# Turned rows of the second MLP chunk in bank 0, and the last attention's gate columns made token by token

## The chip, the cores and the metric

The kernel runs on one NeuronCore of a Trainium2 chip. The metric is the device time of one execution in microseconds (us). Three timed runs of the kernel before are shown, and one further execution was profiled. TensorE is called PE here, its weight loads PEld, VectorE DVE, ScalarE ACT, GpSimd POOL. PSUM has eight banks of 128 x 512 fp32; every matmul writes into one of them, and ACT or DVE reads it from there.

## The reference, cut to what matters

Two blocks run one after the other on 256 tokens of width 1024. Two places matter here: the MLP of the first block and the gates of the last attention of the second block.

```python
# first block, its MLP (16 chunks of 256 hidden columns in the kernel)
h = rmsnorm(x, g_mlp[l])
hid = jnp.square(jax.nn.relu(jnp.einsum("bsd,df->bsf", h, w_mlp_in[l])))
x = x + jnp.einsum("bsf,fd->bsd", hid, w_mlp_out[l])
...
# second block, last attention: 16 heads, 3 gates for each head = 48 columns
h = post_norm(h, 0.5 * swiglu(...), ln_g[layer, 0], ln_b[layer, 0])   # norm 7 in the kernel
qg = h @ w_qg
q = qg[..., :N_HEADS * Dh].reshape(B, S, G, HG, Dh) * (Dh ** -0.5)
gates = jax.nn.sigmoid(qg[..., N_HEADS * Dh:]).reshape(B, S, G, HG, 3)
...
return g_b[..., 0:1] * o_c + g_b[..., 1:2] * o_s + g_b[..., 2:3] * o_w
```

## The kernel before

Everything is kept on the chip; only weights are streamed. Each weight unit (128 x 2048 fp32, or 128 x 384 for the gate columns `("qg", 0)`) is loaded by SP, rounded by ACT into a high part (line 1612) and completed by DVE with a low part (line 2103). A product is then made in three matmuls for each of the eight 128-row pieces of the 1024 inputs: high by high, high by low, low by high. Hence a product over all inputs is 24 matmuls of one form.

There are two forms. `up_T_split` keeps the weights stationary and moves the 256 tokens (`hT_hi`, `hT_lo`), and its result has features as rows. `up_tok_split` keeps 128 tokens stationary and moves the weight columns, and its result has tokens as rows. `hT_hi` and `hT_lo` are the normed activations turned to feature rows. They are made for each block `b` of 128 tokens and each half `h` of the features: PE turns four 128 x 128 pieces (`turn_rows`, line 811), ACT writes `hT_hi` (line 1667), DVE writes `hT_lo` (line 2215). `normed(n, b, k)` makes PE wait for the half that piece `k` belongs to.

Each engine runs its own hand-written order of instructions, and semaphores tie them together. The planner `plan_tiles` gives every PSUM tile a bank by its name. Most names take banks 0 to 3 in turn; some have a bank of their own. `open_tile(name)` makes PE wait until the tile that held this bank before has been read; `tile_copied(engine, name)` waits until the tile itself has been read.

Place one is the start of the first block's MLP, `mlp(2)`. The first two chunks are made token by token, so their hidden rows must be turned afterwards: `turn_hidden(c)` turns `hid` into the tile `("hm", c)`, ACT reads it (line 1800) and DVE reads it again (line 2479). The order on PE is: product down of chunk 0, `turn_hidden(1)`, the one small product `("rel",)` of 33 x 383 for a table, then the product up of chunk 2 into the tile `("m", 2)`. The chunk tiles `("m", c)` have bank `c % 3`, and `("hm", c)` has bank `3 - c`. So `("hm", 1)` and `("m", 2)` share bank 2.

Place two is the start of the last attention. After the last product of the swiglu, PE makes two small tiles `("ck",)` and `("cv",)` (4 and 32 small fp32 products; each fp32 product is two records in the trace), turns the two halves of token block 1 (`rest_of_norm(7)`), makes the 48 gate columns, and goes on to eight query tiles `queries(i)`. The gate columns are made by `up_T_split` as 48 rows of 256 tokens, in tile `("qg",)`. ACT applies tanh (line 1982) into `nsa_gT`. After `queries(3)` PE turns this back to token rows (`gate_rows`, tile `("qt",)`, two transposes of 48 x 128), and DVE finishes the gate from there (line 2751).

Of the kernel before, what the change touches and what calls it, by code (L numbers as in the profile page):

```python
# [29 lines left out]
P = 128  # L30
# [100 lines left out]
def plan_tiles():  # L131
# [7 lines left out]
    def half_norm(n, b):  # L139
        return [("n", n, b, h) for h in range(2)]  # L140
# [30 lines left out]
    third = ffn(2)  # L171
    names += [("cr", 0)] + [("ch", 0, m) for m in range(2)] + third[0:2]
    names += [("cr", 1)] + [("ch", 1, m) for m in range(2)] + third[2:]
    names += half_norm(7, 0) + [("ck",), ("cv",)] + half_norm(7, 1)

    def probs(i):
        return [("pt", i, p) for p in range(4)]

    names += [("qg",)] + [("q", i) for i in range(4)] + [("qt",), ("q", 4), ("cs", 0), ("q", 5)] + probs(0)
    names += [("q", 6), ("ct", 0), ("ov", 0), ("q", 7), ("cs", 1)]  # L180
    for i in range(1, N_PAIR):
        names += probs(i) + [("ov", i)]
# [4 lines left out]
    for seq, name in enumerate(names):  # L187
        if name[0] == "m":
            bank = name[1] % MLP_BODY
        elif name[0:2] == ("n", 2):  # L190
            bank = 2 + name[3]
        elif name[0] == "hm":
            bank = 3 - name[1]
        elif name[0] == "rel":
            bank = 3
        elif name[0] == "vec":
            bank = 5
        elif name == ("cr", 1):
            bank = 4
        elif name[0:2] == ("ch", 1):  # L200
            bank = 5 + name[2]
        elif name[0] == "ov" and name[1] < N_PAIR - 3:
            bank = 7
        else:
            bank, turn = turn % 4, turn + 1
        out[name] = (bank, held[bank], seq)
        held[bank] += 1
# [119 lines left out]
def two_blocks(nc, t, out):  # L327
    ctx = ExitStack()
    with ctx:
# [73 lines left out]
        def take(at, *shape, of=None):  # L403
            n = int(np.prod(shape))
            a = (arena if of is None else of)[:, at[0]:at[0] + n]
            at[0] += n
            if len(shape) == 1:
                return a
            names = "abcd"[:len(shape)]
            return a.rearrange("p (%s) -> p %s" % (" ".join(names), " ".join(names)),  # L410
                               **{x: s for x, s in zip(names[:-1], shape[:-1])})
# [61 lines left out]
        sc = take(at, 2, NB, 8, 16)  # L473
        cw2 = take(at, 2, 2, HD)
        nsa_g = take(at, NB, 3 * NH)
        nsa_gT = take(at, S)[0:3 * NH, :]

# [64 lines left out]
        def frees(name):  # L544
            return tile_read[TILES[name][0]]
# [238 lines left out]
        def _(pe):  # L784
# [12 lines left out]
            def open_tile(name):  # L797
                b, held, _ = TILES[name]
                if held:
                    pe.wait_ge(tile_read[b], held)  # L800
                return banks[b]

            def have(name):
                if name in SPLITS:
                    pe.wait_ge(split_ready, AHEAD + SPLITS[name] + 1)
                else:
                    u = UNITS[name]
                    pe.wait_ge(arrived[u % SLOTS], arrival(u))
# [9 lines left out]
            def up_T_split(o, unit, c0, n, norm=None, act=both_hT):  # L818


                for k in range(KT):
                    if norm is not None:
                        normed(norm, NB - 1, k)
                    for w, a, start, stop in passes(k, KT - 1):
                        ins = mm(o, unit[w][:, k, c0:c0 + n], act[a][:, k, :], start, stop)
                        if start:
                            settle(ins)
                return ins
# [508 lines left out]
            def rest_of_norm(n):  # L1337
                for h in range(2):
                    turn_rows(n, 1, h)
# [100 lines left out]
                                 m == 0, m == 1)  # L1440
            ins.then_inc(tile_done, 1)

            rest_of_norm(7)

            have(("qg", 0))
            o = open_tile(("qg",))
            up_T_split(o[0:3 * NH, 0:S], parts(("qg", 0), KT), 0, 3 * NH, 7).then_inc(tile_done, 1)
            owed[0] += 1

            def queries(i):  # L1450
# [1 line left out]
                o = open_tile(("q", i))  # L1452
                up_T_split(o[:, 0:S], parts(("q", i // 2), KT), i % 2 * P, P).then_inc(tile_done, 1)
                owed[0] += i % 2

            def gate_rows():
                tile_copied(pe, ("qg",))
                o = open_tile(("qt",))
                for b in range(NB):
                    ins = turn(o[:, b * 3 * NH:(b + 1) * 3 * NH], nsa_gT[:, b * P:(b + 1) * P], 3 * NH)  # L1460
                    settle(ins)
                ins.then_inc(tile_done, 1)

            def pair_scores(i, b):
                if b == 0:
# [69 lines left out]
            queries(0)  # L1535
            queries(1)
            queries(2)
            for name in (("kT", 2, 1), ("kT", 4, 1), ("kv", 5, 1), ("ck",), ("cv",)):
                tile_copied(pe, name)
            for k in (2, 3):  # L1540
                pe.wait_ge(k_swapped[k], 32)
            for b in range(NB):
                pair_scores(0, b)
            queries(3)
            gate_rows()
            queries(4)
            for b in range(NB):
                pair_scores(1, b)
# [38 lines left out]
        def _(act):  # L1587
# [391 lines left out]
                                     ACT.Copy)  # L1979
            ins.then_inc(frees(("cv",)), 1)  # L1980
            o = tile_ready(act, ("qg",))
            act.activation(nsa_gT, o[0:3 * NH, 0:S], ACT.Tanh, scale=0.5).then_inc(frees(("qg",)), 1)

            def queries(i):
                copy_tile(("q", i), qT[:, i, :], scale=HD ** -0.5)
# [81 lines left out]
        def _(dve):  # L2067
# [679 lines left out]
            for b in range(NB):  # L2747
                pair_maxima(0, b)
            low_unit(("q", 3))
            o = tile_ready(dve, ("qt",))  # L2750
            dve.tensor_scalar(nsa_g.rearrange("p b c -> p (b c)"), o[:, 0:NB * 3 * NH], 1.0, 0.5,
                              ALU.add, ALU.mult).then_inc(frees(("qt",)), 1)
            tile_copied(dve, ("qt",))
            dve.wait_ge(fills, 5)
            for b in range(NB):
                pair_maxima(1, b)
# [182 lines left out]
```

## Time and profile before

| | us |
|---|---|
| timed runs, median (lowest, highest) | 1442.28 (1440.83, 1442.69) |
| span of the profiled execution | 1440.7 |
| PE busy in it | 1414.5 |
| DVE busy in it | 933.1 |
| ACT busy in it | 659.0 |
| POOL busy in it | 76.9 |

The span runs from the first to the last instruction of the one profiled execution; the timed runs are other executions. The span is 1.5 us below the median of the timed runs. A row of a timeline gives the start, the time from the first start to the last end of what it merges, the engine and line, the operation, what it writes and reads, how many, and in square brackets how long the engine had been idle and who released it. A single matmul is shown for longer than it holds the array, since matmuls follow each other in a pipeline; the distance of two starts is its price.

### The profile page before, as it was taken

How to read it: one execution, taken by the hardware profiler on the slowest of the kernel's cores; microseconds unless marked ns; L12 is line 12 of the kernel's file. 1: busy time of each engine (PE TensorE's matmuls, PEld its weight loads, DVE VectorE, ACT ScalarE, POOL GpSimd, SP SyncE). 2: the span in 40 equal slices, each digit the busy share in tenths (PEclk: the TensorE clock that was granted, in tenths of full speed). 3: DMA queues.
4: the chain of work that ended last, by engine and by line, in shares of the span. 5: the costliest groups of instructions: out<-in, count | busy, mean ns of one | idle time of the engine just before them, and what ended most of it. 6: DMA issues, size and time to landing. Idle time of an engine off the chain costs nothing.

```text
span 1440.7 us, 25236 instructions
## 1 busy us (share of the span) xinstructions
PE 1414.5 (98%) x10426; PEld 1296.3 (90%) x10426; DVE 933.1 (65%) x1372; ACT 659.0 (46%) x833; POOL 76.9 (5%) x73
## 2 busy tenths in 40 slices
PE   8999999999999999999999999999999999999997
PEld 7989978989899999999889999999999887899996
DVE  6878586555665555758875556665555667755556
ACT  5665544343443444453343344444433468543432
POOL 0000140000100000000020000100000200100000
PEclk9999999999999999999999999999999999999999
DMA  8444564775657767564465656766656530566551
GB/s 276 151 133 128 192 205 155 226 235 188 206 188 238 260 199 224 176 191 165 162 208 188 202 187 210 252 198 206 204 177 202 156 118 27 178 207 199 191 188 59
DMA packets 191525, 268.41 MB, mean 186 GB/s; under 512 B 5740, under 2 KB 164752, under 8 KB 191182
## 3 DMA queue, kind: packets, MB, share of 16 engines
q1 hardware_dynamic: 186336, 250.05, 54.0%
q0 software_dynamic: 4224, 15.91, 3.2%
q10 hardware_dynamic: 878, 1.21, 0.3%
q8 instruction: 64, 1.05, 0.3%
q14 instruction: 23, 0.19, 0.0%
HBM read 261.92 MB, written 4.19 MB: 185 GB/s over the span
## 4 chain that ended last, share of the span: by engine, by line
PE 89%; DVE 7%; ACT 3%; issue 1%; DMA 1%; POOL 0%; SPq 0%; DVEq 0%
PE bank L788 87%; PE bank L811 2%; DVE split L2103 1%; DVE resid L2197 1%; DVE resid L2205 1%; DVE stats L2171 1%; DVE resid L2166 1%; DMA ring<-in_w_in 1%; ACT split L1612 1%; ACT arena L1993 0%; ACT act_out L2002 0%; ACT act_out L1635 0%; ACT arena L1685 0%; ACT xn L1993 0%; DVE hT_lo L2215 0%
## 5 line engine op out<-in xcount | busy, mean ns | idle before, releaser
L2103 DVE TENSOR_TENSOR split<-ring,split 128x2048 fp32r<-128x2048 f32 x217 | 496.1, 2289 | 341.0 <-ACT split L1612 340.5
L788 PE MATMUL bank<-hT_hi,split 128*128 128x256 f32 (+1 forms) x3984 | 700.5, 278 | 1.3 <-DVE hid_lo L2479 0.7
L788 PEld LDWEIGHTS bank<-hT_hi,split 128*128 128x128 f32 (+1 forms) x3984 | 607.7, 188 | 8.9 <-issue 4.7
L1612 ACT ACTIVATE split<-ring 128x2048 fp32r<-128x2048 f32 (+1 forms) x224 | 428.0, 1912 | 320.4 <-PE bank L788 315.1
L788 PE MATMUL bank<-hT_lo,split 128*128 128x256 f32 (+1 forms) x1992 | 552.1, 277 | 0.0
L788 PEld LDWEIGHTS bank<-hT_lo,split 128*128 128x128 f32 (+1 forms) x1992 | 374.5, 188 | 2.3
L788 PE MATMUL bank<-split,hid_hi 128*128 128x512 f32 x992 | 285.9, 394 | 0.1
L788 PEld LDWEIGHTS bank<-split,hid_hi 128*128 128x128 f32 x992 | 182.5, 188 | 38.0 <-issue 0.8
L788 PE MATMUL bank<-split,hT_hi 128*128 128x256 f32 (+1 forms) x896 | 172.2, 292 | 2.6 <-DVE hT_lo L2148 1.2
L788 PE MATMUL bank<-split,hid_lo 128*128 128x512 f32 x496 | 158.0, 392 | 0.0
L788 PEld LDWEIGHTS bank<-split,hT_hi 128*128 128x128 f32 x896 | 140.6, 188 | 10.1 <-issue 3.8
L788 PE MATMUL bank<-split,hT_lo 128*128 128x256 f32 (+1 forms) x448 | 127.1, 289 | 0.0
L1787 ACT ACTIVATE act_out<-bank 128x256 f32<-128x256 f32 (+1 forms) x104 | 43.5, 418 | 182.3 <-PE bank L788 182.2
L788 PEld LDWEIGHTS bank<-split,hid_lo 128*128 128x128 f32 x496 | 93.3, 188 | 20.6
L788 PEld LDWEIGHTS bank<-split,hT_lo 128*128 128x128 f32 x448 | 84.2, 188 | 1.9
L2805 POOL TENSOR_TENSOR split<-ring,split 128x2048 fp32r<-128x2048 f32 x7 | 32.6, 4663 | 736.1 <-ACT split L1612 519.6
L2449 DVE TENSOR_TENSOR hid_lo<-hid,hid_hi 128x256 fp32r<-128x256 f32 (+1 forms) x112 | 51.4, 459 | 3.8
L788 PE MATMUL bank<-arena 64*128 64x256 f32 (+6 forms) x442 | 50.2, 321 | 1.2 <-DVE neg_max L2688 0.8
L2548 DVE SCALAR_TENSOR_TENSOR hid<-act_out,bank 128x256 f32<-128x256 f32 x82 | 34.3, 419 | 24.0 <-ACT act_out L1787 24.0
L788 PEld LDWEIGHTS bank<-arena 64*128 64x128 f32 (+3 forms) x442 | 36.6, 168 | 11.2 <-issue 3.7
L2447 DVE CAST hid_hi<-hid 128x256 fp32r<-128x256 f32 (+1 forms) x112 | 34.8, 311 | 3.8
L1667 ACT ACTIVATE hT_hi<-bank 128x512 fp32r<-128x512 f32 x28 | 16.8, 599 | 39.9 <-PE bank L811 39.9
(217 smaller groups left out, 927.5 us busy)
## 6 DMA issues: line engine op xcount, KB each, us to landing
ring<-in_ffn_w SPq DMA_DIRECT2D x132, 1024.0 KB, 5.3
ring<-in_w_in SPq DMA_DIRECT2D x19, 1024.0 KB, 5.5
ring<-in_w_mlp_in SPq DMA_DIRECT2D x16, 1024.0 KB, 5.9
ring<-in_w_mlp_out SPq DMA_DIRECT2D x16, 1024.0 KB, 5.0
ring<-in_sgu_w_in SPq DMA_DIRECT2D x16, 1024.0 KB, 5.5
ring<-in_sgu_w_out SPq DMA_DIRECT2D x8, 1024.0 KB, 4.9
ring<-in_kv_w SPq DMA_DIRECT2D x6, 1024.0 KB, 6.2
ring<-in_w_out SPq DMA_DIRECT2D x4, 1024.0 KB, 5.3
```

The costliest lines, as they stand in the source:

```text
L788: ins = pe.matmul(o, lhsT, rhs, start=start, stop=stop)
L811: return pe.transpose(o, a, ident[0:n, 0:n])
L1612: act.activation(halves(q if i is None else q + BODY, n)[0], ring[:, u % SLOTS, 0:n], ACT.Copy).then_inc(hi_ready, 1)
L1667: act.activation(hT_hi[:, 4 * h:4 * h + 4, b * P:(b + 1) * P], o[:, :].rearrange("p (k s) -> p k s", k=4), ACT.Copy).then_inc(hT_rounded, 1)
L1787: act.activation(act_out[:, b, 0:cols], banks[b][:, 0:cols], func).then_inc(act_ready, 1)
L2103: dve.tensor_tensor(lo, ring[:, u % SLOTS, 0:n], hi.bitcast(F32), ALU.subtract).then_inc(split_ready, 1)
L2166: link(dve.scalar_tensor_tensor(out=r, in0=r, scalar=ALPHA if n >= 4 else 1.0, in1=acc[2 * b + h][:, :], op0=ALU.mult, op1=ALU.add))
L2171: link(dve.bn_stats(stats[:, b, h, :], resid[:, b, h * 512:(h + 1) * 512]))
L2447: dve.tensor_copy(hi, raw).then_inc(hid_rounded, 1)
L2449: return dve.tensor_tensor(lo, raw, hi.bitcast(F32), ALU.subtract)
L2548: dve.scalar_tensor_tensor(out=raw, in0=act_out[:, b, 0:S], scalar=0.5, in1=banks[b][:, S:2 * S], op0=ALU.mult, op1=ALU.mult).then_inc(til ...
L2805: pool.tensor_tensor(lo, ring[:, u % SLOTS, :], hi.bitcast(F32), ALU.subtract).then_inc(split_ready, 1)
```

## The change

The tile `("hm", 1)` gets bank 0 and not bank 2. `("hm", 0)` keeps bank 3.

The gate columns are made in the other form. The 128 tokens of a block are stationary and the 48 weight columns move, 24 matmuls for each of the two blocks, into columns 0 to 47 and 48 to 95 of one tile, in bank 4. The part for block 0 stands ahead of `rest_of_norm(7)`, the part for block 1 behind it. ACT's tanh reads the tile once and writes the gates where they stay. The transposes, their tile `("qt",)` and the buffer `nsa_gT` are gone, and DVE finishes the gates in place in SBUF, at the same place of its order. The name `("qg",)` and `("qt",)` no longer take one of the banks 0 to 3 in turn, so the tiles behind them move to other banks.

```diff
-    names += half_norm(7, 0) + [("ck",), ("cv",)] + half_norm(7, 1)
+    names += half_norm(7, 0) + [("ck",), ("cv",)] + half_norm(7, 1) + [("qg",)]
...
-    names += [("qg",)] + [("q", i) for i in range(4)] + [("qt",), ("q", 4), ("cs", 0), ("q", 5)] + probs(0)
+    names += [("q", i) for i in range(4)] + [("q", 4), ("cs", 0), ("q", 5)] + probs(0)
...
         elif name[0] == "hm":
-            bank = 3 - name[1]
+            bank = 0 if name[1] else 3
...
-        elif name == ("cr", 1):
+        elif name in (("cr", 1), ("qg",)):
             bank = 4
...
+            have(("qg", 0))
+            gates = open_tile(("qg",))
+            up_tok_split(gates[:, 0:3 * NH], parts(("qg", 0), KT), 3 * NH, 0, 7)
             rest_of_norm(7)
-
-            have(("qg", 0))
-            o = open_tile(("qg",))
-            up_T_split(o[0:3 * NH, 0:S], parts(("qg", 0), KT), 0, 3 * NH, 7).then_inc(tile_done, 1)
+            up_tok_split(gates[:, 3 * NH:6 * NH], parts(("qg", 0), KT), 3 * NH, 1, 7).then_inc(tile_done, 1)
             owed[0] += 1
...
-            def gate_rows():
-                tile_copied(pe, ("qg",))
-                o = open_tile(("qt",))
-                for b in range(NB):
-                    ins = turn(o[:, b * 3 * NH:(b + 1) * 3 * NH], nsa_gT[:, b * P:(b + 1) * P], 3 * NH)
-                    settle(ins)
-                ins.then_inc(tile_done, 1)
...
-            for name in (("kT", 2, 1), ("kT", 4, 1), ("kv", 5, 1), ("ck",), ("cv",)):
+            for name in (("kT", 2, 1), ("kT", 4, 1), ("kv", 5, 1), ("ck",), ("cv",), ("qg",)):
                 tile_copied(pe, name)
...
             queries(3)
-            gate_rows()
             queries(4)
...
             o = tile_ready(act, ("qg",))
-            act.activation(nsa_gT, o[0:3 * NH, 0:S], ACT.Tanh, scale=0.5).then_inc(frees(("qg",)), 1)
+            act.activation(nsa_g.rearrange("p b c -> p (b c)"), o[:, 0:NB * 3 * NH], ACT.Tanh,
+                           scale=0.5).then_inc(frees(("qg",)), 1)
...
-            o = tile_ready(dve, ("qt",))
-            dve.tensor_scalar(nsa_g.rearrange("p b c -> p (b c)"), o[:, 0:NB * 3 * NH], 1.0, 0.5,
-                              ALU.add, ALU.mult).then_inc(frees(("qt",)), 1)
-            tile_copied(dve, ("qt",))
+            tile_copied(dve, ("qg",))
+            link(dve.tensor_scalar(nsa_g, nsa_g, 1.0, 0.5, ALU.add, ALU.mult))
```

PE at place one, before: the four transposes of `("hm", 1)` and the first matmuls of chunk 2 (bank2), with the table product between them.

```order
L811 MATMUL bank2<-const,hid 128x128 [waits tile_read2,tile_read1]
L811 MATMUL bank2<-const,hid 128x128 x3
L788 MATMUL bank3<-arena 128x383 [waits tile_read3,rel_wide_ready,rel_in]
L788 MATMUL bank2<-hT_hi,split 128x256 [waits tile_read2,split_ready]
L788 MATMUL bank2<-hT_lo,split 128x256
```

The same rows after the change (the line numbers are one lower there).

```order
L810 MATMUL bank0<-const,hid 128x128 [waits tile_read0,tile_read1]
L810 MATMUL bank0<-const,hid 128x128 x3
L787 MATMUL bank3<-arena 128x383 [waits tile_read3,rel_wide_ready,rel_in]
L787 MATMUL bank2<-hT_hi,split 128x256 [waits tile_read2,split_ready]
L787 MATMUL bank2<-hT_lo,split 128x256
```

Nothing changes its place in the row. Only the bank of the transposes is another, and with it the reader that `tile_read2` of chunk 2 stands for.

PE at place two, before: the small products of `("cv",)` (32x64), the eight transposes of token block 1 (from `resid`), and the start of the gate rows (48x256).

```order
L788 MATMUL bank1<-arena 32x64 x31
L811 MATMUL bank2<-const,resid 128x128 [waits tile_read2,xn_ready]
L811 MATMUL bank2<-const,resid 128x128 x3
L811 MATMUL bank3<-const,resid 128x128 [waits tile_read3,xn_ready]
L811 MATMUL bank3<-const,resid 128x128 x3
L788 MATMUL bank0<-hT_hi,split 48x256 [waits tile_read2,tile_read0,split_ready]
L788 MATMUL bank0<-hT_lo,split 48x256
```

The same place after: the end of the gate columns of block 0, the transposes, and the start of those of block 1 (both 128x48).

```order
L787 MATMUL bank4<-split,hT_hi 128x48
L810 MATMUL bank2<-const,resid 128x128 [waits tile_read2,xn_ready]
L810 MATMUL bank2<-const,resid 128x128 x3
L810 MATMUL bank3<-const,resid 128x128 [waits tile_read3,xn_ready]
L810 MATMUL bank3<-const,resid 128x128 x3
L787 MATMUL bank4<-split,hT_hi 128x48 [waits tile_read2]
L787 MATMUL bank4<-split,hT_lo 128x48
```

24 matmuls of 128x48 now stand between the small products and the transposes, and 24 more behind the transposes take the place of the 24 of 48x256. The two 48-wide transposes between `queries(3)` and `queries(4)` are gone.

## Rows read from the trace of the kernel before

**Rows 1.** The page: span, busy time of the engines, and the chain by engine.

```profile
span 1440.7 us, 25236 instructions
PE 1414.5 (98%) x10426; PEld 1296.3 (90%) x10426; DVE 933.1 (65%) x1372; ACT 659.0 (46%) x833; POOL 76.9 (5%) x73
...
PE 89%; DVE 7%; ACT 3%; issue 1%; DMA 1%; POOL 0%; SPq 0%; DVEq 0%
```

**Rows 2.** Waits of PE: engine, line, for whom: total us, times, longest.

```profile
PE bank L811 <- DVE resid L2205: 3.2, 6, 0.9
...
PE bank L788 <- DVE hid_lo L2479: 0.7, 1, 0.7
```

**Rows 3.** Timeline at the second MLP chunk's turning.

```profile
235.58 0.60 PE L811 MATMUL bank<-const,hid 128*128 128x128 f32 x4
236.11 0.91 PE L788 MATMUL bank<-arena 33*128 33x383 f32 x2
236.22 0.60 ACT L1800 ACTIVATE hid_hi<-bank 128x512 fp32r<-128x512 f32 x1 [4.79 <-PE bank L811]
...
236.91 0.69 DVE L2479 TENSOR_TENSOR hid_lo<-bank,hid_hi 128x512 fp32r<-128x512 f32 x1 [1.94 <-ACT hid_hi L1800]
237.75 0.36 PE L788 MATMUL bank<-hT_hi,split 128*128 128x256 f32 x1 [0.73 <-DVE hid_lo L2479]
```

**Rows 4.** DVE's timeline ahead of that: the low part of chunk 2's weights.

```profile
229.88 2.29 DVE L2103 TENSOR_TENSOR split<-ring,split 128x2048 fp32r<-128x2048 f32 x1 [0.16 <-DVE hid_lo L2479]
```

**Rows 5.** Timeline: the small products, the turning of block 1, the gate rows.

```profile
1141.59 3.02 PEld L788 LDWEIGHTS bank<-arena 128*32 128x32 f32 x64 [0.17 <-issue]
1141.62 0.69 DVE L2215 TENSOR_TENSOR hT_lo<-bank,hT_hi 128x512 fp32r<-128x512 f32 x1
...
1145.70 0.66 PE L811 MATMUL bank<-const,resid 128*128 128x128 f32 x4 [0.93 <-DVE resid L2205]
1146.34 0.75 DVE L2205 SCALAR_TENSOR_TENSOR resid<-resid,rstd,gain_rows 128x512 f32<-128x512 f32 x1
1146.39 0.60 ACT L1667 ACTIVATE hT_hi<-bank 128x512 fp32r<-128x512 f32 x1 [1.85 <-PE bank L811]
1147.02 0.69 DVE L2215 TENSOR_TENSOR hT_lo<-bank,hT_hi 128x512 fp32r<-128x512 f32 x1
...
1147.15 0.83 PE L811 MATMUL bank<-const,resid 128*128 128x128 f32 x4 [0.79 <-DVE resid L2205]
...
1147.86 0.42 PE L788 MATMUL bank<-hT_hi,split 128*48 128x256 f32 x1
1148.02 0.60 ACT L1667 ACTIVATE hT_hi<-bank 128x512 fp32r<-128x512 f32 x1 [1.03 <-PE bank L811]
...
1148.65 0.69 DVE L2215 TENSOR_TENSOR hT_lo<-bank,hT_hi 128x512 fp32r<-128x512 f32 x1 [0.93 <-ACT hT_hi L1667]
```

**Rows 6.** DVE's timeline: the low part of the gate columns' weights (128 x 384).

```profile
1124.64 0.55 DVE L2103 TENSOR_TENSOR split<-ring,split 128x384 fp32r<-128x384 f32 x1
```

**Rows 7.** Stretches: length, busy (count) of PE, PEld, DVE, ACT, POOL, clock granted, DMA.

```profile
9.94:11.14 1.20, 1.20 (x11) 1.14 (x11) 0.92 (x2) 0.06 (x2) 0.00 (x0) 0.50 0.42 52
...
44.99:48.40 3.41, 2.12 (x18) 1.70 (x17) 2.19 (x1) 3.38 (x8) 0.00 (x0) 1.00 0.00 0
...
1144.61:1147.50 2.89, 1.17 (x10) 0.77 (x9) 2.79 (x6) 0.60 (x1) 0.11 (x1) 1.00 0.00 0
1147.50:1150.91 3.41, 3.41 (x18) 2.93 (x17) 2.48 (x3) 2.84 (x6) 2.78 (x4) 0.50 0.63 225
1150.91:1154.00 3.09, 3.09 (x29) 3.09 (x28) 0.63 (x1) 2.19 (x3) 0.00 (x0) 1.00 0.97 280
```

**Rows 8.** PE's timeline: last gate rows, first query matmuls; then around the gates' turning.

```profile
1150.43 0.41 PE L788 MATMUL bank<-hT_hi,split 128*48 128x256 f32 x1
1150.64 0.41 PE L788 MATMUL bank<-hT_lo,split 128*48 128x256 f32 x1
...
1151.93 0.39 PE L788 MATMUL bank<-hT_hi,split 128*48 128x256 f32 x2
1152.15 0.28 PE L788 MATMUL bank<-hT_lo,split 128*128 128x256 f32 x1
...
1165.51 0.28 PE L788 MATMUL bank<-hT_hi,split 128*128 128x256 f32 x1
1165.72 0.32 PE L811 MATMUL bank<-const,arena 48*128 48x48 f32 x2
1165.97 0.39 PE L788 MATMUL bank<-hT_hi,split 128*128 128x256 f32 x1
1166.19 0.28 PE L788 MATMUL bank<-hT_lo,split 128*128 128x256 f32 x1
```

**Rows 9.** PE's timeline: 128 stationary columns, 32 moving, later in the attention.

```profile
1189.88 1.84 PE L788 MATMUL bank<-arena 128*128 128x32 f32 x15
```

**Rows 10.** PE's timeline at the start, clock 0.50: transposes of two shapes.

```profile
8.07 1.94 PE L811 MATMUL bank<-const,xn 128*128 128x128 f32 x8 [2.63 <-DVE xn L2128]
9.94 1.27 PE L811 MATMUL bank<-const,shared_rows 19*128 19x19 f32 x10
```

**Rows 11.** ACT's timeline: gate tanh, and the later stretch where ACT leads.

```profile
1152.24 0.38 ACT L1982 ACTIVATE arena<-bank 48x256 f32<-48x256 f32 x1 [0.90 <-PE bank L788]
1152.52 1.91 ACT L1612 ACTIVATE split<-ring 128x2048 fp32r<-128x2048 f32 x1
...
1197.82 1.74 ACT L2002 ACTIVATE act_out<-bank 128x256 f32<-128x256 f32 x4 [0.62 <-PE bank L811]
```

More of the change, by code:

```diff
@@ L475, in two_blocks @@
         nsa_g = take(at, NB, 3 * NH)
-        nsa_gT = take(at, S)[0:3 * NH, :]
         rel_dram = nc.dram_tensor("rel_scratch", (NH, P, N_REL), F32, kind="Internal")
```

## The prediction

> **What bounds the kernel now.** I read the page first: PE is busy for 98% of the span and holds 89% of the chain that ended last [rows 1]. So time goes away only where PE stands still, works at a lower clock, or does less; work of ACT and DVE counts where it makes PE wait. The second view is the list of PE's waits [rows 2]. Two of its rows belong to this change: one wait of 0.7 us for the low part of hidden rows (line 2479), and the waits of transposes for the last norm step (line 2205). The third view is the timeline at these places [rows 3, 5, 8]. The fourth is the table of stretches with the granted clock [rows 7], which shows something that no wait shows: behind the turning of block 1 PE works for 3.41 us at a clock of 0.50, its lower level of 1.2 GHz, and is back at 2.4 GHz at 1150.9.
>
> **Part one, bank of the second chunk's turned rows.** The table product starts as two records at 236.11; the two take 0.91 us as shown, to 237.02. The first matmul of chunk 2 starts at 237.75, after 0.73 us of idle time that DVE's line 2479 ended [rows 3]. That instruction reads the turned rows from bank 2 (236.91 to 237.60), and chunk 2 writes bank 2. With the turned rows in bank 0 nothing of chunk 2's start depends on it. What is late next? The weights of chunk 2 were ready at 229.88 + 2.29 = 232.17 [rows 4], their tokens long before, so the next limit is PE itself. The table product's own pipeline lets its follower start slightly before its shown end, so the gain is between 0.73 and 0.8; I take **0.8 us off**. The transposes now need bank 0, whose tile was read before the turning itself could start (the hidden rows that are turned come from it or from its neighbour, chunk 1), so no wait takes the place. ACT and DVE read the same number of elements as before. The down product of chunk 1 needs this low part, but only after 48 matmuls of chunk 2, more than 5 us later.
>
> **Part two, the turning of the gates.** The last matmul of `queries(3)` starts at 1165.51, the two transposes stand at 1165.72, and the next query tile starts at 1165.97, with its second matmul at 1166.19 [rows 8]. Where query matmuls follow gate matmuls without a change of kind, the distance is 0.11 (1151.93 for two, then 1152.15) [rows 8]. So the turning costs 1165.97 - 1165.51 - 0.11 = 0.35 us, and 0.22 - 0.12 = 0.10 more in the slow first step behind it. **0.45 us off.** DVE's part (once from PSUM, now in SBUF) and ACT's tanh (0.38 us, [rows 11]) shrink or stay, and ACT waited 0.90 us for it. Both stay beside PE's work: no price.
>
> **Part three, the gate columns in the other form.** Before, 24 matmuls; after, 48, each with 128 stationary and 48 moving columns. No row of before has just that shape. The nearest is 128 stationary with 32 moving: 15 of them in 1.84 us, less some 0.28 for the last one's length, is 1.56 / 14 = **0.112 us each** [rows 9]. The other neighbour is 32 stationary with 64 moving: 64 in 3.02 us, 0.047 each [rows 5]. The first has the new one's stationary width, and its 32 columns alone cannot need 0.112, so it is the load that sets the pace; I take 0.112 and keep 0.047 for a rival.
>
> The Trainium skill (TensorE: Matmul & The Clock Gate, LDWEIGHTS) says the load's time goes with the number of stationary columns, not with the contraction; at its rate 128 columns take 107 ns, and the row agrees. The same page's table of back-to-back gaps puts a matmul of 1 to 64 moving columns at about 25 ns; by that the 48 would cost an estimated 1.2 us instead of 5.4. That is the rival below, priced there from rows.
>
> Now the places. Block 0's 24 take 24 x 0.112 = 2.69 us. Their inputs are there: `hT_lo` of block 0 ended at 1142.31 [rows 5], the weights at 1125.19 [rows 6]. They can start where the small products end; the last of these starts some 0.17 before the end of PE's busy time, 1145.70 - 0.93 = 1144.77 [rows 5]. So they run from 1144.61 to 1147.30. Before, this time held 0.93 + 0.79 us of waiting and four transposes. Both halves of block 1's rows are ready by then (1147.09), so eight transposes at 0.109 run to about 1148.2. Behind them, by the distances of before: ACT started 0.69 after the first of four transposes and 0.60 long; DVE ended at 1147.71, which is 2.01 after them; PE followed 0.15 later. So the first half is usable at 1147.30 + 2.01 + 0.10 + 0.15, about 1149.4-1149.5, and PE idles about 1.2 us. The second half is usable 0.7 later and not waited for, since 12 matmuls take 1.34. Block 1's 24 end at 1149.4 + 2.69 = **1152.1**, where the queries start. Before, they start at 1152.04 [rows 8]. **Against the profiled execution, all at full clock, part three is zero** (0.06).
>
> **What the clock does to this.** Before, the gate matmuls stand 0.21 apart at the low clock (1150.43, 1150.64) and 0.11 at the high one [rows 8]. At full clock they would have begun at 1147.83, waited for the second half (1148.65 + 0.69 + 0.15 = 1149.49) and ended at 1149.49 + 12 x 0.113 = 1150.85. So the low clock costs 1.19 of before's time, and clock against clock the new form is 1.25 us dearer: it does not fill a hole with useful work, it puts 2.7 us of extra work in a hole of 1.7 and opens one of 1.2.
>
> Will the clock fall again? The stretch 1144.61 to 1147.50, ahead of the fall, has PE busy for 1.17 of 2.89 us. A stretch with more transposes (44.99 to 48.40, busy 2.12 of 3.41) kept 1.00 [rows 7]. After the change PE is busy nearly throughout until 1148.2, which speaks for a full clock. Against it: at the start of the program ten transposes with 19 moving columns kept PE busy throughout from 9.94 to 11.14, and the clock stayed at 0.50 [rows 7, 10]. The change makes the stretch from 1144.6 to 1152.1 almost all of such narrow work: 48 narrow matmuls, eight transposes, a hole. I think it likelier that the clock falls again, and later than before, so that full-width query matmuls meet it. A stretch as long as the one before, 3.41 us, at half pace takes 1.7 us of them. The narrow ones lose little: the 19-wide transposes at the low clock stand at most 0.127 apart (1.27 / 10), near the 0.112.
>
> **Sum of the likeliest case:** -0.80 - 0.45 + 1.25 - 1.19 + 1.7 = **+0.5 us**. The profiled execution had the low stretch; its span is 1.5 below the median, which I take for what lies around the span, so I add to the median: 1442.28 + 0.5 = **1442.8 us**. Nothing absorbs it later: after the queries the chain stays on PE. At 1197.82, where ACT takes over the chain for 16 us, it had waited 0.62 for PE [rows 11], so a shift of part two's size passes.
>
> **Rivals.**
> - *The clock stays full.* The narrow matmuls close the hole ahead of the transposes, and the hole behind them is 1.2 us, no more than what 44.99 to 48.40 held (3.41 - 2.12 = 1.29) at full clock [rows 7]. Then -0.80 - 0.45 + 1.25 - 1.19 = -1.2, 1441.1 us.
> - *Narrow matmuls are cheap* (0.047 each). Block 0's end at 1145.74 and hardly delay the transposes; block 1's wait for the second half at about 1149.6 and end 12 x 0.047 later, 1150.15, that is 1.9 earlier than before. Sum -3.15, 1439.1 us. Against it stands the 0.112 of the 32-column row.
> - *Slower: the clock stays low over block 1's gates and a stretch of queries, and the narrow ones double too.* The place is 1149.4 on; full transposes at the low clock stand 0.213 apart (7 steps and one length in 1.94) [rows 10]. It decides from the point where a narrow matmul keeps that pace and not that of the 19-wide ones: 24 x 0.10 = 2.4 more, with 1.7 for the queries: -1.2 + 2.4 + 1.7 = +2.9, 1445.2 us.
> - *Part one brings nothing*, because chunk 2's start has another late input that the same 0.73 hid. Rows 4 speak against it. Then +0.8 on the forecast: 1443.6 us.
>
> **How the numbers follow.** Chances: likeliest case 0.45, full clock 0.32, cheap narrow ones 0.04, slow case 0.09, part one void 0.08, the rest 0.02. A measurement of this kernel can tell about 0.2%, 2.9 us, from no change: below 1439.4 is faster, above 1445.2 slower. Faster: the cheap case and little else, 0.05. Slower: about half of the slow case and a little scatter, 0.06. The rest, 0.89, is no change. The range goes from 1440.2 (the full-clock case, less the 0.9 that the runs of before scatter) to 1444.6 (the likeliest case with two low stretches of full matmuls, 1442.8 + 1.7, and 0.1). It leaves out the cheap case, the slow one and some scatter, about 0.17.
>
> **What would show it.** Part one: chunk 2's first matmul directly behind the table product, no idle for line 2479. Part two: no 48 x 48 transposes, query matmuls 0.11 apart through the seam. Part three: narrow matmuls 0.112 apart, transposes of block 1 some 1.6 us later against the small products, a hole of 1.2 us, queries 7.5 us after the last small product. The clock: one low stretch that begins behind the transposes; none would show the first rival. I am wrong if the narrow matmuls stand far from 0.112, if the hole is not there, or if a wait of ACT or DVE in the attention grows.

## The result, and the profile after

| | before | after |
|---|---|---|
| median, us (6 runs each) | 1442.35 | 1446.22 |
| lowest to highest | 1440.80 to 1442.77 | 1444.75 to 1447.06 |
| span of the profiled execution | 1440.7 | 1444.9 |

The ratio is 1.0032, with a 95% interval of 1.0021 to 1.0043. The kernel became slower by 3.9 us. The forecast was 1442.8 us and no change that can be told; the range ended at 1444.6. The measured 1446.22 also lies above 1445.2, where the prediction had put its bound for "slower" and had given that a chance of 0.06.

The page of the changed kernel has these lines for those of [rows 1]: the span, the busy times and the chain.

```profile
span 1444.9 us, 25267 instructions
PE 1421.4 (98%) x10448; PEld 1302.7 (90%) x10448; DVE 932.7 (65%) x1372; ACT 659.1 (46%) x833; POOL 76.9 (5%) x73
...
PE 87%; DVE 7%; ACT 3%; DMA 1%; issue 1%; POOL 0%; SPq 0%; DVEq 0%
```

PE was busy for 6.9 us more, with only 22 records more on the page. The other engines did the same as before. So work on PE took longer, and the waits do not tell why. In the list of PE's waits the 0.7 us for line 2479 [rows 2] has gone, the waits of transposes for the last norm step fell from 3.2 to 1.0 us, and only 0.6 us stands at the gate columns:

```profile
PE bank L787 <- DVE hT_lo L2206: 0.6, 1, 0.6
```

The table of stretches does tell. Its columns are as in [rows 7].

```profile
1143.32:1146.03 2.71, 2.71 (x27) 2.71 (x25) 2.32 (x4) 0.00 (x0) 0.02 (x1) 1.00 0.02 6
1146.03:1159.68 13.65, 13.09 (x62) 12.69 (x62) 5.87 (x4) 6.41 (x10) 2.86 (x4) 0.50 0.70 233
1159.68:1162.00 2.32, 2.32 (x22) 2.32 (x22) 0.00 (x0) 0.00 (x0) 0.00 (x0) 1.00 0.86 281
```

The clock was at its lower level, 1.2 GHz, for 13.65 us, four times as long as in [rows 7]. Ahead of the fall PE had been busy without a gap, with the 24 narrow matmuls of token block 0. The hole behind the turning comes only at 1147.98, 1.95 us after the fall, so it did not cause the fall. The timeline of PE, ACT and DVE at this place answers to [rows 5, 8]:

```profile
1143.32 0.29 PE L787 MATMUL bank<-split,hT_hi 128*128 128x48 f32 x1
...
1145.90 0.28 PE L787 MATMUL bank<-split,hT_hi 128*128 128x48 f32 x1
...
1146.02 1.97 PE L810 MATMUL bank<-const,resid 128*128 128x128 f32 x8
...
1147.80 0.69 DVE L2206 TENSOR_TENSOR hT_lo<-bank,hT_hi 128x512 fp32r<-128x512 f32 x1 [2.09 <-ACT hT_hi L1657]
...
1148.54 0.41 PE L787 MATMUL bank<-split,hT_hi 128*128 128x48 f32 x1 [0.56 <-DVE hT_lo L2206]
...
1153.47 0.39 PE L787 MATMUL bank<-split,hT_hi 128*128 128x48 f32 x1
1153.68 0.56 PE L787 MATMUL bank<-hT_hi,split 128*128 128x256 f32 x1
1154.04 0.41 PE L787 MATMUL bank<-hT_lo,split 128*128 128x256 f32 x1
```

Block 0's narrow matmuls: 23 steps from 1143.32 to 1145.90 are 0.112 each, as forecast. Block 1's: 23 steps from 1148.54 to 1153.47 are 0.214 each. The queries start at 1153.68 and run at half pace until 1159.68.

At place one the timeline answers to [rows 3]:

```profile
235.12 0.60 PE L810 MATMUL bank<-const,hid 128*128 128x128 f32 x4
235.65 0.91 PE L787 MATMUL bank<-arena 33*128 33x383 f32 x2
236.49 0.38 PE L787 MATMUL bank<-hT_hi,split 128*128 128x256 f32 x1
```

From the first transpose to chunk 2 it is 1.37 us where it was 2.17: 0.80 less.

**Where the time went, trace against trace.** The new trace reaches place one 0.46 earlier, which is not the change's doing. Place one gives 0.80. Between the two places 0.12 is gained. In the attention I measure from the start of the last small product to the start of the first product with 32 moving columns, read off single records: 26.95 us before, 32.55 after, so 5.60 lost. From there on the two agree within 0.02. Together -0.46 - 0.80 - 0.12 + 5.60 = +4.2, the difference of the spans. The 5.60 has three parts. The queries start 10.52 us after the last small product, not 7.48: +3.04. The first three query tiles take from 1153.68 to 1164.65 where they took from 1152.04 to 1160.09: +2.92. The rest of the way, with the seam without the turning, is 0.34 shorter, and the parts add up to 5.62.

### The profile page after: what moved, and what is told of

The parts are those of the page before. It is cut to its first block, busy times and chain, and to the rows that moved or that the text cites. A ratio compares the mean times of both kernels' runs of the same rounds, so it can differ in the third digit from the quotient of the medians.

```text
span 1444.9 us, 25267 instructions
## 1 busy us (share of the span) xinstructions
PE 1421.4 (98%) x10448; PEld 1302.7 (90%) x10448; DVE 932.7 (65%) x1372; ACT 659.1 (46%) x833; POOL 76.9 (5%) x73
## 4 chain that ended last, share of the span: by engine, by line
PE 87%; DVE 7%; ACT 3%; DMA 1%; issue 1%; POOL 0%; SPq 0%; DVEq 0%
PE bank L787 85%; PE bank L810 2%; DVE split L2094 1%; DMA ring<-in_w_in 1%; DVE resid L2188 1%; DVE resid L2196 1%; DVE stats L2162 1%; ACT split L1602 1%; DVE resid L2157 1%; ACT act_out L1625 0%; ACT arena L1984 0%; ACT act_out L1993 0%; ACT xn L1984 0%; DVE hT_lo L2206 0%; DVE shared_rows L2398 0%
## 5 line engine op out<-in xcount | busy, mean ns | idle before, releaser
L787 PE MATMUL bank<-hT_hi,split 128*128 128x256 f32 x3968 | 698.9, 278 | 0.5 <-DVE split L2094 0.4
L787 PEld LDWEIGHTS bank<-hT_hi,split 128*128 128x128 f32 x3968 | 607.5, 189 | 7.7 <-issue 3.7
L787 PE MATMUL bank<-hT_lo,split 128*128 128x256 f32 x1984 | 550.5, 277 | 0.0
L787 PEld LDWEIGHTS bank<-hT_lo,split 128*128 128x128 f32 x1984 | 374.4, 189 | 2.2
L787 PE MATMUL bank<-split,hT_hi 128*128 128x256 f32 (+2 forms) x928 | 179.7, 293 | 2.5 <-ACT act_out L1625 0.6
L787 PEld LDWEIGHTS bank<-split,hT_hi 128*128 128x128 f32 x928 | 147.4, 190 | 10.9 <-issue 3.8
L787 PE MATMUL bank<-split,hT_lo 128*128 128x256 f32 (+2 forms) x464 | 132.2, 290 | 0.0
L787 PEld LDWEIGHTS bank<-split,hT_lo 128*128 128x128 f32 x464 | 88.5, 191 | 1.9
```

The lines of the kernel that those rows point to most:

```text
L787: ins = pe.matmul(o, lhsT, rhs, start=start, stop=stop)
```

## The experiments

Each run was timed beside the kernel before. "Distance" is the one just defined: from the last small product to the first product with 32 moving columns. Before has 26.95, the change 32.55. "Low" is how long the clock was at 0.50 in the profiled execution, without the start and the end of the program.

| run | median us | before, beside it | ratio (95%) | distance | low near the gates |
|---|---|---|---|---|---|
| e1 part one alone | 1439.77 | 1441.47 | 0.9990 (0.9981 to 0.9999) | 27.08 | 3.41 |
| e2 gates alone | 1447.59 | 1441.47 | 1.0038 (1.0025 to 1.0052) | 31.14 | 10.24 |
| e3 wide moving | 1441.33 | 1441.47 | 0.9999 (0.9990 to 1.0008) | 26.84 | none |
| e4 change and fill | 1442.30 | 1441.47 | 1.0004 (0.9995 to 1.0013) | 26.64 | none |
| e5 old form and fill | 1439.64 | 1441.02 | 0.9988 (0.9980 to 0.9997) | 25.64 | none |
| e6 two halves | 1439.32 | 1441.02 | 0.9987 (0.9979 to 0.9996) | 25.05 | none |
| e7 all behind | 1447.10 | 1441.02 | 1.0042 (1.0029 to 1.0055) | 32.45 | 10.24 |
| e8 query first | 1442.70 | 1441.02 | 1.0010 (1.0001 to 1.0019) | 30.07 | 3.41 twice |
| e9 two halves and fill | 1439.86 | 1441.76 | 0.9985 (0.9976 to 0.9994) | 24.98 | none |
| e10 the change again | 1445.30 | 1441.76 | 1.0025 (1.0015 to 1.0034) | 31.12 | 10.24 |

### The two parts apart: e1 and e2

e1 has only this, e2 all but this:

```diff
-            bank = 3 - name[1]
+            bank = 0 if name[1] else 3
```

> The kernel before with part one alone: the turned rows of the second MLP chunk go to bank 0, the gate columns stay as they were. Theory (the whole loss is in the gate columns and the clock behind them): chunk 2's first matmul starts 1.37 us after the first turning transpose, not 2.17, and the time is 0.8 us below the kernel before, about 1441.5; the clock has one low stretch of 3.4 us at the gate rows, or none. Rival (part one also costs something, such as a wait later in the MLP): the time is at or above that of the kernel before.

> The changed kernel with part one undone: only the gate columns are changed. Theory: 0.8 us above the changed kernel, about 1447.0, with the clock low for some 10 to 14 us behind the transposes of token block 1 and the narrow matmuls there 0.213 us apart. Rival (part one carries the loss): about 1442.

e1's timeline at place one shows the 0.80 again (235.70 to 237.06 is 1.36).

```profile
235.70 0.60 PE L811 MATMUL bank<-const,hid 128*128 128x128 f32 x4
236.22 0.91 PE L788 MATMUL bank<-arena 33*128 33x383 f32 x2
237.06 0.39 PE L788 MATMUL bank<-hT_hi,split 128*128 128x256 f32 x1
```

e1's runs fall in two groups, six from 1439.33 to 1439.77 and five from 1440.83 to 1441.22. The profiled one is of the upper group and has the low stretch at the gate rows. That the lower group has none is inferred from its mean clock (0.995 to 0.998 there, 0.994 to 0.996 above, so the two overlap), not seen in a trace of e1. The groups stand 1.5 us apart. Part one is worth its 0.80 in the trace; the medians say 1.7, with an interval of 0.1 to 2.7. e2 carries the whole loss: 6.1 us above its own before, where the changed kernel was 3.9 above its own. The two intervals overlap, so they do not tell whether the difference is more than the 0.8 of part one; e2's trace has a second low stretch, at 214.47 to 217.89. The rival that part one hides a cost is out.

### The same work, but wide: e3

Same places, same number, same stationary operand. What moves is 256 columns of the query weights; the gates are not computed.

```diff
+            have(("q", 0))
...
-            up_tok_split(gates[:, 0:3 * NH], parts(("qg", 0), KT), 3 * NH, 0, 7)
+            up_tok_split(gates[:, 0:UC], parts(("q", 0), KT), UC, 0, 7)
             rest_of_norm(7)
-            up_tok_split(gates[:, 3 * NH:6 * NH], parts(("qg", 0), KT), 3 * NH, 1, 7).then_inc(tile_done, 1)
+            up_tok_split(gates[:, UC:2 * UC], parts(("q", 0), KT), UC, 1, 7).then_inc(tile_done, 1)
```

> The changed kernel with the same 48 matmuls at the same places and the same 128 stationary columns, but each moves 256 columns of the first query weights, not 48 gate columns; the gates are so left out of the result. At full clock both forms should stand 0.112 to 0.114 apart. Theory (a clock that falls and stays low because the matmuls are narrow): the clock is never low there, or for one stretch of 3.4 us, and the time is 1441 to 1442.5. Rival A (the hole of 1.2 us behind the transposes throws the clock): it falls as in the changed kernel and comes back one stretch later, 1443 to 1444. Rival B (the loss is the order of work and not the clock): 1446, as the changed kernel.

The stretches of e3: block 0's matmuls and the transposes, the hole, block 1's matmuls.

```profile
1143.48:1147.00 3.52, 3.52 (x33) 3.52 (x32) 2.33 (x4) 0.05 (x1) 0.82 (x2) 1.00 0.02 5
1147.00:1148.32 1.32, 0.35 (x4) 0.11 (x1) 0.74 (x2) 1.31 (x4) 1.32 (x3) 1.00 0.58 130
1148.32:1151.10 2.78, 2.77 (x23) 2.78 (x24) 2.75 (x2) 2.38 (x4) 0.75 (x1) 1.00 0.87 309
```

The hole is there: PE is busy for 0.35 of 1.32 us. The clock stays at 1.00. With five times the columns the kernel is 4 us faster than with 48, each against its own before. So the hole by itself does not do it, and neither does the order of work (rivals A and B). The price of such work at full clock is also seen: the distance is 26.84. The prediction's terms for full clock give 26.95 - 0.45 + 0.06 = 26.56.

### Full matmuls in the hole: e4

```diff
+            def fill(n, bank):
+                nil = zeros[:, :].bitcast(BF16)
+                for _ in range(n):
+                    settle(mm(bank[:, :], nil[:, 0:P], nil[:, 0:512], True, True))
...
             rest_of_norm(7)
+            fill(5, banks[7])
```

> The changed kernel with five full matmuls on zeros (512 moving columns, about 0.22 us each at full clock) put into the hole behind the transposes of token block 1; the narrow matmuls stay. Theory (the narrow matmuls hold the clock low): the clock still falls near the transposes and is low for 7 to 14 us, 1444.5 to 1446.5. Rival A (the hole throws the clock): it stays at full clock and the time is 1441 to 1442.

My theory missed here. The narrow matmuls are all there, and the clock stayed at 1.00 in the profiled execution. The last two lines are the timeline's: the turning and four of the five matmuls on zeros.

```profile
1143.70:1147.50 3.80, 3.79 (x34) 3.71 (x34) 2.32 (x4) 0.41 (x1) 1.11 (x3) 1.00 0.02 4
1147.50:1151.20 3.70, 3.66 (x29) 3.03 (x28) 3.48 (x3) 3.33 (x7) 1.77 (x2) 1.00 0.92 288
...
1146.40 1.09 PE L810 MATMUL bank<-const,resid 128*128 128x128 f32 x8
1147.54 1.03 PE L787 MATMUL bank<-zeros 128*128 128x512 bf16 x4
```

The eleven runs reach from 1440.84 to 1442.85; some may have had a low stretch. About 1.1 us of full matmuls on zeros made the changed kernel some 3 us faster, each against its own before. How they did it is not shown. They start only about 1147.3, and in the other traces of the changed gates the fall came at 1146.03 (the change), 1147.25 (e10, 0.2 us ahead of its hole) and 1149.73 (e2, 0.2 us into its hole), that is before the hole or hardly in it. In e4's profiled execution the fall stayed away although the work ahead of the zeros was the same as in e10. So the hole is not what brings the clock down in the changed kernel; whether it helps to keep it down is open.

### The place: e7 and e8

e7 puts both blocks' narrow matmuls behind the turning. e8 puts block 1's behind the first query tile.

```diff
 e7
+            rest_of_norm(7)
             up_tok_split(gates[:, 0:3 * NH], parts(("qg", 0), KT), 3 * NH, 0, 7)
-            rest_of_norm(7)
...
 e8
-            up_tok_split(gates[:, 3 * NH:6 * NH], parts(("qg", 0), KT), 3 * NH, 1, 7).then_inc(tile_done, 1)
-            owed[0] += 1
...
             queries(0)
+            up_tok_split(gates[:, 3 * NH:6 * NH], parts(("qg", 0), KT), 3 * NH, 1).then_inc(tile_done, 1)
+            owed[0] += 1
             queries(1)
```

> The changed kernel with the narrow matmuls of token block 0 moved behind the turning of token block 1, so that all 48 stand behind it; the form is that of the change. Theory (a long stretch of narrow matmuls holds the clock low, wherever the hole is): the two waits ahead of the turning are back, the clock falls there, and is low over all 48 narrow matmuls at 0.213 us each and some of the query matmuls: 13 to 17 us low, the distance 34 to 37 us, time 1447 to 1451. Rival (the hole of 1.2 us behind the turning made the loss, and it is filled here): one low stretch of 3.4 us at most, distance 28 to 30, time 1442 to 1443.

> The changed kernel with the narrow matmuls of token block 1 moved behind the first query tile, so that 24 full matmuls stand between the turning and them. Theory (once low, the clock comes back only when full matmuls have run, and the narrow ones only delay that): one low stretch of 3.4 us at most two, the distance from the last small product to the first product with 32 moving columns is 27.5 to 29.5 us where the changed kernel has 32.6, time 1441.5 to 1443.5. Rival (the clock falls on the narrow matmuls alone, so it falls again on the moved ones): a low stretch behind them as well, 30 us or more, 1444 and above.

e7: the turning and its two waits, then the stretches from the first narrow matmuls on.

```profile
1144.85 0.63 PE L810 MATMUL bank<-const,resid 128*128 128x128 f32 x4 [1.14 <-DVE resid L2196]
1146.10 0.66 PE L810 MATMUL bank<-const,resid 128*128 128x128 f32 x4 [0.62 <-DVE resid L2196]
...
1146.40:1148.38 1.98, 1.98 (x21) 1.98 (x20) 1.40 (x3) 1.57 (x4) 1.98 (x4) 1.00 0.25 95
1148.38:1158.62 10.24, 10.24 (x50) 10.24 (x50) 2.91 (x2) 3.86 (x5) 0.85 (x2) 0.50 0.83 290
```

There is no hole behind the turning here, and the clock was low all the same, for 10.24 us in which PE was busy without a gap. The rival that the hole made the loss is out. What brought the clock down in this run is not told apart, since the waits ahead of the turning are back (1.14 and 0.62 us), as before the change. No idle time kept it down. My own numbers were too high (13 to 17 us low, distance 34 to 37): the first narrow matmuls still ran at full clock, and the distance is 32.45. e8's stretches, and from the timeline the first of the moved narrow matmuls:

```profile
1148.17:1151.59 3.42, 3.42 (x19) 3.42 (x18) 2.30 (x2) 1.95 (x3) 0.37 (x1) 0.50 0.96 271
1151.59:1155.00 3.41, 3.41 (x32) 3.41 (x32) 0.00 (x0) 0.00 (x0) 0.00 (x0) 1.00 1.01 375
1155.00:1158.41 3.41, 3.41 (x18) 3.41 (x18) 1.06 (x1) 2.44 (x3) 0.00 (x0) 0.50 0.45 179
...
1152.26 0.19 PE L787 MATMUL bank<-split,hT_hi 128*128 128x48 f32 x1
```

The first low stretch ran over query matmuls, and the clock was back at 1151.59. The 24 narrow ones stand in the middle stretch (from 1152.26 to the start of the next query tile at 1154.86), PE is busy for all of it, and the clock falls again at 1155.00. This is the rival's case: narrow matmuls bring the clock down with no idle time near them. The first fall, at 1148.17, has idle time ahead of it. No narrow matmuls ran while the clock was low, and the distance is 2.5 us shorter than the change's. The median of 1442.70 lies in the range of my theory, though, and the rival had asked for 1444 and above: the runs reach from 1440.37 to 1445.26, nearly as wide as e10's and wider than all others', and the profiled one is among the slower ones. That executions differ in how many of the two falls they meet fits this, and is not shown.

The traces also say how long the clock stayed down. It came back when the query matmuls had run for 6.0 us in the changed kernel, 4.4 in e2, 3.9 in e10, 3.6 in e7 and 3.8 in e8's first stretch. In the first four of these, the narrow matmuls behind the fall had been done at half pace before that.

### The old form kept warm, and in two halves: e5, e6, e9

e5 is part one and zeros in the two waits of the turning. e6 is part one and the old form cut in two blocks of tokens, one at the change's new place. e9 is e6 with two matmuls on zeros behind the turning.

```diff
 e5
-            rest_of_norm(7)
+            fill(4, banks[4])
+            turn_rows(7, 1, 0)
+            fill(3, banks[4])
+            turn_rows(7, 1, 1)
...
 e6
+            def gate_half(b):
+                unit = parts(("qg", 0), KT)
+                for k in range(KT):
+                    normed(7, b, k)
+                    for w, a, start, stop in passes(k, KT - 1):
+                        ins = mm(o[0:3 * NH, b * P:(b + 1) * P], unit[w][:, k, 0:3 * NH],
+                                 both_hT[a][:, k, b * P:(b + 1) * P], start, stop)
...
+            gate_half(0)
+            rest_of_norm(7)
+            gate_half(1).then_inc(tile_done, 1)
```

> The kernel before with part one, the gate rows in their old form and at their old place, and seven full matmuls on zeros (512 moving columns) in the two waits of the turning: four ahead of its first half, three ahead of its second. Theory (the old form loses 1.2 us to one low stretch of the clock, and work in the holes ahead of it keeps the clock): no low stretch there, and the distance from the last small product to the first product with 32 moving columns is 25.8 to 26.2 us where it was 26.95 before; time 1439.3 to 1440.3, without the upper group of runs near 1441 that part one alone has. Rival (the clock falls by something else than a lack of full matmuls): one low stretch as before, 27 us, and up to 0.4 more for the fillers.

> The kernel before with part one, and the gate columns in the old form (48 stationary columns, tokens move) but in two halves of 128 tokens, one ahead of the turning of token block 1 and one behind. So the place is that of the change and the form is the old one; the turning of the gates stays. Theory (what hurts is 128 stationary for 48 moving columns, not the place): 24 matmuls of 48 stationary and 128 moving columns take some 0.056 us each, 1.35 us, and fill the hole ahead of the turning; no low stretch; the distance from the last small product to the first product with 32 moving columns falls to 25.0 to 26.3 us, time about 1439. Rival (the place hurts: the transposes start later and open a hole behind them): 27 us or more and the clock falls. Open: whether a matmul of this type keeps its pace with 128 moving columns; if it needs 0.11, the distance is 27 to 28.

> The kernel with the gate columns in two halves of the old form (48 stationary columns, 128 tokens move, part one kept) and two full matmuls on zeros between the turning of token block 1 and the second half. Theory (a low stretch is left there in some executions and accounts for the upper group of runs at 1440.3 to 1441.1): the upper group shrinks and the lowest runs stay near 1438.6; median 1438.7 to 1439.3. Rival (the upper group comes from low stretches elsewhere, as at the products with 32 moving columns): two groups as without the fillers, median 1439 to 1440.

e5's distance is 25.64, 1.3 below before. So the 1.2 us that the prediction had put on the low stretch of before were about right. But its runs still reach 1441.31, and its profiled execution shows another low stretch later, which starts in the row of products with 128 stationary and 32 moving columns:

```profile
1168.75:1170.33 1.58, 1.58 (x15) 1.58 (x15) 1.51 (x11) 1.58 (x9) 0.00 (x0) 1.00 0.00 0
1170.33:1173.74 3.41, 3.41 (x18) 3.41 (x18) 3.09 (x12) 1.00 (x5) 0.00 (x0) 0.50 0.00 0
```

This stretch was at full clock in the trace before. So this place, too, meets a fall in some executions and not in others.

e6's timeline shows the cheaper form in the hole: the first and the last of block 0's 24 matmuls, then the transposes.

```profile
1143.26 0.26 PE L788 MATMUL bank<-hT_hi,split 128*48 128x128 f32 x1
...
1144.67 0.22 PE L788 MATMUL bank<-hT_hi,split 128*48 128x128 f32 x1
1144.73 0.61 PE L811 MATMUL bank<-const,resid 128*128 128x128 f32 x4
1145.70 0.66 PE L811 MATMUL bank<-const,resid 128*128 128x128 f32 x4 [0.36 <-DVE resid L2216]
```

23 steps in 1.41 us are 0.061 each, half of the change's 0.112, with the same arithmetic. Its distance of 25.05 is the shortest but for e9's 24.98. e6 is faster than before by 0.13% (0.04% to 0.21%) and faster than the change by 0.45%, against each one's own kernel before. The pace goes with what moves here: 48 stationary and 256 moving columns stood 0.113 apart in the kernel before, 128 moving ones 0.061. e6's profiled execution is one of its lower group (1438.85) and has no low stretch. e9 cannot be told from it: the lowest run is 1438.39 against 1438.59, and the upper runs at 1440 to 1441 are still there. The fillers do not remove them, which speaks for the rival that they come from elsewhere; e9's own trace has a low stretch at 214.24 to 217.65, far ahead of the gates. There PE had just waited 1.87 us, and the matmuls of that place are wide (512 moving columns), so narrow matmuls are not the only thing that goes ahead of a fall.

### The change again: e10

> The changed kernel once more, beside the others of this call. Theory: 1444.7 to 1447.1 as before, with a low stretch of 10 to 14 us in the profiled execution over the narrow matmuls of token block 1 and the queries behind them, and the narrow ones 0.213 us apart in it. Rival (its slow time was an accident of when the executions ran): some runs near 1441 to 1442.5.

Nine of ten runs lie from 1444.76 to 1447.28, one at 1442.33. The low stretch of the profiled execution:

```profile
1147.25:1157.49 10.24, 9.31 (x44) 9.08 (x43) 4.83 (x4) 5.69 (x9) 1.97 (x3) 0.50 0.92 307
```

So the loss belongs to the kernel, and how large it is differs between executions: the clock was low for 13.65 us in the first trace and for 10.24 here, with distances of 32.55 and 31.12. The narrow matmuls of block 1 ran at the low clock in both.

## Why the prediction was wrong, point by point

- **Part one** was right: 0.8 forecast, 0.80 in the trace of the change, of e1 and of all others that have it.
- **Part two** was right. From the last matmul of `queries(3)` to the second of the next tile it is 0.24 us where it was 0.68, so 0.44 saved for 0.45 forecast. The query tile ahead of the seam took 0.10 longer in the changed kernel's trace (23 steps in 2.81 us for 2.71), which leaves the 0.34 above.
- **Part three at full clock** was right. At full clock (e4) the narrow matmuls stand 0.112 apart, the block 0 ones end where they were put, the hole behind the turning is there (0.98 us in e3, 1.07 in e8), and the full-clock distance (26.64 in e4) is within 0.1 of what 26.95 - 0.45 + 0.06 gives. One sum is off as written: 1147.30 + 2.01 + 0.10 + 0.15 is 1149.56, not 1149.4 to 1149.5. Block 1's narrow matmuls started 4.91 us after the last small product in e4, which would be 1149.47, so the slip cost nothing.
- **The cheap case** did not come: the 0.112 of [rows 9] held. The Trainium skill (TensorE: Matmul & The Clock Gate, LDWEIGHTS) has the load's time go with the number of stationary columns. At full clock the 0.112 for 128 columns agrees; at its rate 48 columns would take an estimated 40 ns, and no run shows that, since e6's 0.061 goes with its 128 moving columns. The gap of about 25 ns that the same page of the Trainium skill (Back-to-back issue gap) has for few moving columns was shown by no run.
- **What the clock does** was right in direction and failed in size. The prediction took one low stretch of 3.41 us, as long as that of before, and put it on full query matmuls: 1.7 us. It was 13.65 us in the profiled execution and 10.24 in e2, e7 and e10, and the queries lost 2.92 us and not 1.7. The term "a stretch as long as the one before, 3.41 us, at half pace" is the step that failed. It held the length fixed where the work in the stretch had changed: before, the clock was back after 3.41 us, in which matmuls of 256 moving columns ran, and after, it did not come back while narrow ones ran, and then only 6.0 us into the queries.
- **"The narrow ones lose little"** failed as well. The row of the 19-wide transposes [rows 10], which have only 19 active rows, did not carry over; why they keep their pace is shown by no run. The narrow matmuls went to 0.214, as the full transposes of the same rows do. Block 1's took 5.14 us (1148.54 to 1153.68) for 2.69 forecast: 2.45 us. They also started 0.5 later than forecast, since the eight transposes took 1.97 us at the low clock; the hole behind them shrank to 0.56. The slow rival had both steps and was priced at 1445.2; I gave it 0.09 and took only one stretch in it too, so the price was also short, by some 1 us.
- **The sum with the measured terms:** -0.80 - 0.34, then +3.04 and +2.92 at the gates and queries, which is +4.8; 0.12 was gained between the places, and the trace started 0.46 earlier. The medians say +3.9 in the first comparison, and e10 has +3.5. Against the forecast of this stretch (1.25 - 1.19 + 1.7 = 1.76) the measured 5.96 is 4.2 too much: 2.45 for the narrow matmuls, 0.5 for their late start, 1.2 for the queries.
- **"Nothing absorbs it later"** was right: behind the first 32-column product the two traces agree within 0.02 us.

That the clock falls and stays low with the narrow matmuls is shown by e3 (wider ones in the same places, no fall, and eleven runs at most 1443.16), e7 (no hole behind the turning, a long low stretch), and by the change's own trace and e8 (a fall behind narrow ones with PE busy throughout). That idle time ahead of a fall can do it too is what before, e7 and e9 suggest. What stays open is why e4's 1.1 us of zeros sufficed in its profiled execution, and how often it does.

## What to carry to other kernels

Before a small product is turned round, compare the two forms by what must be loaded and what moves: 48 stationary and 128 moving columns took 0.061 us, 128 stationary and 48 moving 0.112, for the same arithmetic. A hole on PE is only worth filling with work that would cost its time anyway, as e6 does with half of the old form. A row of matmuls that load much and move little can bring the clock down with PE busy throughout, as in e8; then every step of PE in that stretch costs about double, that of the narrow matmuls too (0.214 for 0.112). When a low stretch is priced, ask what will run in it after the change, not how long it was before.

## What the runs showed of the hardware

- PE busy throughout did not keep the full clock. In e8 PE was busy for 3.41 of 3.41 us at 1.00, with 24 matmuls of 128 stationary and 48 moving columns in it, and the clock was 0.50 behind it; in e7 it stayed at 0.50 for 10.24 us of unbroken work, of which the first 6.7 us were narrow matmuls.
- At the lower level those matmuls stood 0.214 us apart, at the higher one 0.112 (both in the changed kernel's trace). With 48 stationary and 128 moving columns it was 0.061 at the higher level (e6).
- Executions of one kernel fall in groups 1.5 us apart (e1: 1439.5 and 1441.1). One low stretch of 3.41 us fits that in size, since half of it is 1.7 us; the profiled executions of the upper groups of e1 and e5 have one and that of e6's lower group has none. An engineer who compares two medians within 0.1% here may be comparing how often each met such a stretch.
